# A two-layer hybrid encoder step: another order of projections and heads in the mixer, masks in spare rows, Silu on ScalarE, scaling on GpSimd

## The chip, the cores and the metric

The kernel runs on one core of a Trainium2 chip. The metric is device time in microseconds (us) of one execution. Before the change three runs gave 1753.67 us as median (1753.1 to 1754.33).

## The reference, cut to what matters

320 rows (256 of a prompt, 64 of a running stream) go through two layers. Each layer reads one wide projection of its normalised input and feeds three groups with it:

```
xn = rmsnorm(x, g_mix)
qa, ka, va, ga, ra, bb, cb, hb, qc, kc, vc = split_cols(xn @ w_in)     # 3088 columns
y_a = rmsnorm(gla(qa*48**-.5, ka, va, log_sigmoid(ga@w_g2 + b)/16), g_gla) * silu(ra)
y_b = bb * conv3(cb*hb)
a   = softmax(q1 k1) - lam * softmax(q2 k2)      # q, k: rmsnorm, then rotary; 4 heads x 2 parts
y_c = rmsnorm(a @ vc, g_sub) * (1 - lam_init)    # prompt rows see keys up to their own chunk of 64
x   = x + concat(y_a, y_b, y_c) @ w_out
x   = x + ffn(rmsnorm(x, g_ffn))                 # layer 0: dense SwiGLU; layer 1: top 2 of 8 experts
```

Outputs are the rows, and the keys, values, recurrent states and convolution histories of both streams. All is float32.

## The kernel before, in words

Activations lie transposed: 1024 features in 8 blocks of 128 partitions, 320 tokens in the free dimension (`xR`). Each weight block of 128 columns, a *cut* of 128x1024, is loaded by SyncE into a ring of three slots, split by ScalarE into a rounded high part (`hi`, L757) and by VectorE into the rest (`lo`, L1103). TensorE multiplies three products of high and low parts, 8 blocks by 3 = 24 matmuls of 320 columns (`features`, `three`, L1707 is the matmul helper, L1710 the transpose helper). A cut is made three cuts ahead of its use. A layer has 25 projection cuts and 8 output cuts (`wo_cut`, also 24 matmuls each).

PSUM banks are dealt out as rings whose jobs are listed ahead (`JOBS`): C and T have two banks, S two, O and D one. A job may begin when the job one ring length before it has been emptied. Every engine runs its own list, written out by hand, and all waits are semaphore counts; the order of the lists is the order in `build`.

The mixer of a layer goes, on TensorE: `kc` (3 cuts), `qc` (3), `qa` (2), `ka` (2), `vc` (3), with transposes back to rows (`rows_T`), sums of squares (`square_sums`), the spread of the row norms (`spread_rstd`), the gate logits and the transposes of rotated keys and queries (`heads_T`) between them. Then a loop over 12 heads (3 row tiles by 4 heads) with one projection cut in each round as filling (`FILL`: `va`, `ra`, `bb`, `cb`, `hb`), and rounds that also take a piece of the recurrent group (`inner`, `update`, `recurrent`). A head is `scores` (on TensorE), maximum and its negative (VectorE), two exponentials (ScalarE), the difference of the two softmaxes (VectorE), transpose and product with the values (TensorE). Then the rows of both groups are transposed (`transposed`), gated, split and multiplied with `w_out`.

What the change touches: the mask of the scores was an own matmul of one row, `C("rowsel")` times `C("neg")`, in `scores`. The gate `silu(ra)` was an exponential on ScalarE (`ra_exp`) and add, reciprocal and product on VectorE (`swish`, L1322 to L1324). Rows were scaled by their reciprocal roots on VectorE (`scaled`, L1159); GpSimd only computed the roots (`rsqrt`, L588 and L589) and added the squares of the input (`add_squares`, L595 and L598). `decays` and `decayed` prepare the recurrent group. The gains `g_gla` and `g_sub` were broadcast over partitions with a matmul of one row (`bcast`) and multiplied in row form.

Of the kernel before, what the change touches and what calls it, by code (L numbers as in the profile page):

```python
# [24 lines left out]
P = 128  # L25
# [33 lines left out]
for _name, _w in [("ident", 128), ("tri", 128), ("ones", 128), ("scan", T), ("cc", NT * DK), ("ss", NT * DK),  # L59
                  ("tok", NT), ("iota8", 8), ("slot", MAXB * P), ("attm", H * CH), ("rowsel", P), ("neg", CH)]:  # L60
    CONST[_name] = (_at, _w)
    _at += _w
# [20 lines left out]
for _l in range(DEPTH):  # L83
# [5 lines left out]
    for _n, _c in (("vc", VC), ("va", VA), ("ra", RA)):  # L89
        _unit(("in", _l, _c, 256), [(_n, _l, 0), (_n, _l, 1)])  # L90
        _unit(("in", _l, _c + 256, 128), [(_n, _l, 2)])
    for _n, _c in (("bb", BB), ("cb", CB), ("hb", HB)):
        _unit(("in", _l, _c, 256), [(_n, _l, 0), (_n, _l, 1)])
    for _c in range(2):
        for _j in range(2):
            _unit(("wo", _l, _c, _j), [("wo", _l, _c, 2 * _j), ("wo", _l, _c, 2 * _j + 1)])
# [48 lines left out]
FILL = ["va", "va", "va", "ra", "ra", "ra", "bb", "bb", "cb", "cb", "hb", "hb"]  # L145
JOBS = {r: [] for r in "CTSOD"}
JOBS["T"] += [("par",), ("bcast", 0)]
JOBS["D"] += [("bcast", 1)]
for _k in range(KB):
    JOBS[XT_RING[_k]].append(("xt", _k))  # L150
for _l in range(DEPTH):
    JOBS["C"] += [c[2:] for c in CUTS[KC0[_l]:KC0[_l] + N_IN]]
    JOBS["C"] += [("ya", _l, t) for t in range(NT)] + [("yc", _l, t) for t in range(NT)]
    JOBS["T"] += [("tok", "kc", _l, c) for c in range(3)] + [("tok", "qc", _l, c) for c in range(3)]
    JOBS["T"] += [("pk", _l), ("tok", "vc", _l, 0), ("kt", _l, 0), ("kt", _l, 1), ("kt", _l, 2), ("tok", "vc", _l, 1)]
    JOBS["T"] += [("qt", _l, t) for t in range(NT)] + [("tok", "vc", _l, 2)]
    for _n in range(HEADS + 2):
        if 1 <= _n <= 3:
            JOBS["T"].append(("tok", "va", _l, _n - 1))
        if _n == 2:  # L160
            JOBS["T"] += [("kd", _l, t) for t in range(NT)]
        if _n >= 2:
            JOBS["T"].append(("at", _l, _n - 2))
    JOBS["S"] += [("s", _l, n) for n in range(HEADS)]
    JOBS["O"] += [("oc", _l, t) for t in range(NT)]
    JOBS["D"] += [("ss", 2 * _l), ("R", 2 * _l), ("gl", _l, 0), ("gl", _l, 1), ("att", _l, 0), ("att", _l, 1)]
    JOBS["D"] += [("U", _l, 0), ("U", _l, 1), ("U", _l, 2)] + [("oa", _l, t) for t in range(NT)]
# [59 lines left out]
def build(nc, A, O):  # L227
# [5 lines left out]
    with ExitStack() as ctx:  # L233
# [34 lines left out]
        pcol = sb("pcol", [P, 48])  # L268
        bc = sb("bc", [P, 960])
# [33 lines left out]
        bgla = bc[:, 576:768].rearrange("p (l d) -> p l d", l=DEPTH)  # L303
        bsub = bc[:, 768:960].rearrange("p (l d) -> p l d", l=DEPTH)
# [39 lines left out]
        era = [glaf[:, 3 * T:4 * T], glaf[:, 6 * T:7 * T]]  # L344
        bbs = glaf[:, 4 * T:6 * T].rearrange("p (b n) -> p b n", b=2)
        yv = glaf[:, 6 * T:6 * T + 2 * (T + 2)].rearrange("p (b n) -> p b n", b=2)
        brow, prow = glaf[0:1, 0:960], glaf[0:48, 960:960 + P]
# [5 lines left out]
        atm = mb("atm", [P, 256])  # L353
# [6 lines left out]
        mx = mb("mx", [P, 2, 2])  # L360
        nm = mb("nm", [P, 2, 2])
        sm = mb("sm", [P, 2, 2])
        rc = mb("rc", [P, 2])
        rc2 = mb("rc2", [P, 1])
# [59 lines left out]
        const_in, prow_in, brow_in, x_in, w_small = sem("const_in"), sem("prow_in"), sem("brow_in"), sem("x_in"), sem("w_small")  # L424
# [10 lines left out]
        bcast_ready, tables_ready, lam_exp = sem("bcast_ready"), sem("tables_ready"), sem("lam_exp")  # L435
# [3 lines left out]
        ln_ready, d_ready, exps_ready, gk_ready = sem("ln_ready"), sem("d_ready"), sem("exps_ready"), sem("gk_ready")  # L439
        rope_ready, conv_ready = sem("rope_ready"), sem("conv_ready")  # L440
        era_ready, ya_ready, yc_ready = sem("era_ready"), sem("ya_ready"), sem("yc_ready")
        swish_ready, silu_ready, yhi_ready, ylo_ready = sem("swish_ready"), sem("silu_ready"), sem("yhi_ready"), sem("ylo_ready")
        nm_ready, am_ready = sem("nm_ready"), sem("am_ready")
# [11 lines left out]
        heads_order = [("oc", 0), ("oa", 0), ("oa", 1), ("oc", 1), ("oa", 2), ("oc", 2)]  # L455
# [57 lines left out]
        def _(sp):  # L513
# [15 lines left out]
            sp.wait_ge(const_in, 16)  # L529
            sp.wait_ge(x_in, 32)  # L530
            for l in range(DEPTH):
                sp.dma_start(wga[:, l], A["w_in"][l, :, GA:GA + GR].rearrange("(k p) n -> p k n", p=P)).then_inc(wga_in, 16)
            for n, u in enumerate(UNITS):
                src, (b, w) = source(u)
# [39 lines left out]
        def _(pool):  # L574
# [15 lines left out]

            def add_squares(i, o):
# [43 lines left out]
            pool.wait_ge(bcast_ready, 1)  # L635
            hd = DK // 2
            for l in range(DEPTH):
                for w in range(2):
# [3 lines left out]
                    nc.gpsimd.tensor_tensor(SG[:, l, w, :, hd:DK], ssn[:, :, hd:DK], g[:, 0:hd].unsqueeze(1).to_broadcast([P, NT, hd]), ALU.mult)  # L642
                last = nc.gpsimd.tensor_scalar(bsub[:, l], bsub[:, l], 1.0 - LAM0[l], None, ALU.mult)
# [23 lines left out]
            for l in range(DEPTH):  # L667
# [4 lines left out]
                for what in ("kc", "qc"):  # L672
# [3 lines left out]
                    if what == "kc":  # L676
                        keys_out(l)
                for what, t in heads_order:
                    pool.wait_ge(ss_ready, ss_count(l, what, t))
                    rsqrt(rs_slot(l, what, t), TILES[t][1], DV, 4)  # L680
                    if (what, t) == ("oa", 0):
                        states_out(l)
                    if (what, t) == ("oa", 2):
                        history_out(l)
# [44 lines left out]
        def _(act):  # L729
            step = Steps(act, act_step)  # L730
            hs_n = [0]
            act.dma_start(const[:], A["const"]).then_inc(const_in, 16)
            act.dma_start(xhat[:, 0:2, :], A["x_prompt"][0].rearrange("(t p) d -> p t d", p=P)).then_inc(x_in, 16)
            act.dma_start(xhat[0:DEC, 2, :], A["x_sample"][0]).then_inc(x_in, 16)
            at = 0
            for name in ("g_q", "g_k", "lambda_q1", "lambda_k1", "lambda_q2", "lambda_k2", "g_gla", "g_sub"):
                n = DEPTH * A[name].shape[1]
                act.dma_start(brow[0:1, at:at + n], A[name].rearrange("l d -> (l d)").unsqueeze(0)).then_inc(brow_in, 16)
                at += n

# [33 lines left out]
            nc.scalar.copy(pcol[:], RT.bank(("par",))[:, 0:48]).then_inc(RT.free, 1)  # L774
            act.wait_ge(RT.full, RT.filled(("bcast", 0)))
            nc.scalar.copy(bc[:, 0:480], RT.bank(("bcast", 0))[:, 0:480]).then_inc(RT.free, 1)
            act.wait_ge(RT.free, 2)
# [4 lines left out]
            for o in range(KB):  # L782
                x_square(0, o)

            act.wait_ge(lam_exp, 1)
            nc.scalar.activation(lamt[:], lamt[:], ACT.Exp).then_inc(lam_exp, 1)

            for l in range(DEPTH):
# [32 lines left out]
                def squares_oa(t):  # L821
                    rows = TILES[t][1]
                    act.wait_ge(RD.free, RD.emptied(("oa", l, t)))
                    squares(Ya[0:rows, t], rows)
# [1391 lines left out]
```

## Time and profile before

| quantity | value |
|---|---|
| median of 3 runs | 1753.67 us |
| the profiled execution's own time | 1753.11 us |
| its span, first to last instruction | 1751.2 us |
| TensorE busy, share of the span | 93% |
| VectorE, ScalarE, GpSimd busy | 74%, 56%, 8% |
| mean granted TensorE clock | 0.949 of full |

The span is what the core's instructions cover; the profiled time has 1.9 us around it. Busy TensorE time comes from modelled ends, so what counts is the idle time and the granted clock of each stretch. In the views by stretch the columns are: stretch and its length, then the busy time (and number of instructions) of TensorE, its weight loads, VectorE, ScalarE and GpSimd, then the granted TensorE clock as a share of full speed, the busy share of the DMA engines, and GB/s.

### The profile page before, as it was taken

The page shows a single profiled execution, that of the slowest core. Times are in us where ns is not written, and L with a number is a line of the kernel's source. Part 1 is how long each engine was busy: PE and PEld are TensorE (multiplying, and loading weights), DVE is VectorE, ACT ScalarE, POOL GpSimd, SP SyncE. Part 2 cuts the span into 40 slices and gives each one's busy share as a digit, 9 for nine tenths or more (in the row PEclk, how much of TensorE's full clock was granted, in tenths as well). Part 3 has the DMA queues.
Part 4 walks back from the last instruction along what each step waited for, and adds up shares of the span by engine and source line. Part 5 has one row for each costly group of instructions (what it writes and reads, how often), then busy time and mean ns, then how long its engine had stood idle before and what let it go on. Part 6 is the DMA issues. An engine that isn't in the chain of part 4 may idle for free.

```text
span 1751.2 us, 21767 instructions
## 1 busy us (share of the span) xinstructions
PE 1626.5 (93%) x8526; PEld 1392.5 (80%) x8526; DVE 1291.2 (74%) x1346; ACT 987.4 (56%) x1042; POOL 144.7 (8%) x181
## 2 busy tenths in 40 slices
PE   5979789999987897889999999999999999999994
PEld 3867689999987686768888888888888888888883
DVE  3656756665447376578888888888888888888885
ACT  3443243333334333357777777777777777777772
POOL 5400211000013002100000000000000000000001
PEclk8988889999999797889999999999999999999997
DMA  5322139444433220399999999999999999999993
GB/s 157 105 93 73 52 108 312 145 150 152 156 109 95 84 73 29 128 360 365 359 383 374 358 389 365 365 385 363 373 381 367 370 375 356 389 370 362 386 364 102
DMA packets 230054, 450.13 MB, mean 257 GB/s; under 512 B 10178, under 2 KB 72336, under 8 KB 229952
## 3 DMA queue, kind: packets, MB, share of 16 engines
q1 hardware_dynamic: 214944, 420.64, 67.4%
q10 hardware_dynamic: 10944, 17.13, 2.7%
q0 software_dynamic: 4064, 10.96, 2.0%
q8 instruction: 69, 1.13, 0.3%
q14 instruction: 33, 0.27, 0.0%
HBM read 431.22 MB, written 17.47 MB: 256 GB/s over the span
## 4 chain that ended last, share of the span: by engine, by line
PE 84%; DVE 9%; ACT 3%; issue 1%; DMA 1%; POOL 1%; POOLq 0%; ACTq 0%; SPq 0%; DVEq 0%
PE bank L1707 27%; PE bank L2128 12%; PE bank L2127 12%; PE bank L2132 12%; PE bank L2138 6%; PE bank L2147 6%; PE bank L2141 6%; DVE cut_lo L1103 2%; PE bank L1710 1%; ACT cut_hi L757 1%; PE bank L2156 1%; POOL acc L598 1%; DVE G L1610 0%; DMA xhat<-x_sample 0%; DVE t L1159 0%
## 5 line engine op out<-in xcount | busy, mean ns | idle before, releaser
L1619 DVE TENSOR_TENSOR split_lo<-raw,split_hi 128x2048 fp32r<-128x2048 f32 x336 | 768.2, 2291 | 129.1 <-ACT split_hi L1020 128.2
L1020 ACT CAST split_hi<-raw 128x2048 fp32r<-128x2048 f32 x336 | 640.5, 1910 | 265.7 <-PE bank L2132 167.8
L2127 PE MATMUL bank<-split_hi,xgT_hi 128*128 128x512 f32 x896 | 359.4, 401 | 3.9 <-DVE xgT_lo L1643 3.9
L2128 PE MATMUL bank<-split_hi,xgT_lo 128*128 128x512 f32 x896 | 356.3, 398 | 0.0
L757 ACT CAST cut_hi<-ring 128x1024 fp32r<-128x1024 f32 x124 | 129.1, 1046 | 274.8 <-PE bank L1707 266.1
L1707 PE MATMUL bank<-xT_hi,cut_hi 128*128 128x320 f32 x752 | 250.0, 332 | 0.5 <-DVE xT_lo L1117 0.5
L2132 PE MATMUL bank<-split_lo,xgT_hi 128*128 128x512 f32 x896 | 246.3, 397 | 0.0
L1707 PE MATMUL bank<-xT_hi,cut_lo 128*128 128x320 f32 x752 | 243.1, 323 | 0.0
L1707 PE MATMUL bank<-xT_lo,cut_hi 128*128 128x320 f32 x752 | 242.9, 323 | 0.0
L1103 DVE TENSOR_TENSOR cut_lo<-ring,cut_hi 128x1024 fp32r<-128x1024 f32 x124 | 152.6, 1235 | 115.4 <-ACT cut_hi L757 115.1
L2127 PEld LDWEIGHTS bank<-split_hi,xgT_hi 128*128 128x128 f32 x896 | 169.2, 189 | 43.5 <-DVE xgT_lo L1643 4.3
L2132 PEld LDWEIGHTS bank<-split_lo,xgT_hi 128*128 128x128 f32 x896 | 169.3, 189 | 41.3
L2128 PEld LDWEIGHTS bank<-split_hi,xgT_lo 128*128 128x128 f32 x896 | 169.5, 189 | 39.5
L1707 PEld LDWEIGHTS bank<-xT_hi,cut_hi 128*128 128x128 f32 x752 | 151.3, 201 | 6.0 <-issue 3.0
L1707 PEld LDWEIGHTS bank<-xT_lo,cut_hi 128*128 128x128 f32 x752 | 152.5, 203 | 0.0
L1707 PEld LDWEIGHTS bank<-xT_hi,cut_lo 128*128 128x128 f32 x752 | 152.1, 202 | 0.0
L2138 PE MATMUL bank<-split_hi,hmT_hi 128*128 128x512 f32 x448 | 142.1, 398 | 0.0
L2141 PE MATMUL bank<-split_hi,hmT_lo 128*128 128x512 f32 x448 | 139.1, 391 | 0.0
L2147 PE MATMUL bank<-split_lo,hmT_hi 128*128 128x512 f32 x448 | 121.8, 393 | 0.0
L2141 PEld LDWEIGHTS bank<-split_hi,hmT_lo 128*128 128x128 f32 x448 | 84.1, 188 | 19.8
L2147 PEld LDWEIGHTS bank<-split_lo,hmT_hi 128*128 128x128 f32 x448 | 84.0, 188 | 19.4
L2138 PEld LDWEIGHTS bank<-split_hi,hmT_hi 128*128 128x128 f32 x448 | 82.3, 188 | 16.9
(263 smaller groups left out, 1633.0 us busy)
## 6 DMA issues: line engine op xcount, KB each, us to landing
raw<-moe_w_gate SPq DMA_DIRECT2D x112, 1024.0 KB, 8.2
raw<-moe_w_up SPq DMA_DIRECT2D x112, 1024.0 KB, 7.6
raw<-moe_w_down SPq DMA_DIRECT2D x112, 1024.0 KB, 5.3
ring<-w_in SPq DMA_DIRECT2D x16, 1024.0 KB, 5.3
ring<-ffn_w_gate SPq DMA_DIRECT2D x11, 1024.0 KB, 5.6
ring<-ffn_w_up SPq DMA_DIRECT2D x11, 1024.0 KB, 5.3
ring<-ffn_w_down SPq DMA_DIRECT2D x10, 1024.0 KB, 5.0
ring<-w_out SPq DMA_DIRECT2D x8, 1024.0 KB, 5.0
```

The lines of the kernel that those rows point to most:

```text
L598: nc.gpsimd.tensor_tensor(acc[:], acc[:], sqx[:, o % 2], ALU.add).then_inc(acc_ready, 1)
L757: nc.scalar.copy(split_cut(cut_hi, q), raw_cut(q)).then_inc(cut_hi_ready, 1)
L1020: return nc.scalar.copy(split_hi[:, i % SR, :], raw[:, (i % PR) * PIECE:(i % PR + 1) * PIECE]).then_inc(hi_ready, 1)
L1103: V.tensor_tensor(split_cut(cut_lo, q), raw_cut(q), split_cut(cut_hi, q).bitcast(F32), ALU.subtract).then_inc(cut_lo_ready, 1)
L1619: V.tensor_tensor(split_lo[:, i % SR, :], raw[:, (i % PR) * PIECE:(i % PR + 1) * PIECE], split_hi[:, i % SR, :].bitcast(F32), ALU.subtract ...
L1707: return TE.matmul(out, lhsT, rhs, start=start, stop=stop)
L2127: TE.matmul(o, xgT_hi[:, kk, :], hi[:, c], start=kk == 0, stop=False)
L2128: TE.matmul(o, xgT_lo[:, kk, :], hi[:, c], start=False, stop=False)
L2132: last = TE.matmul(o, xgT_hi[:, kk, :], lo[:, 512 * k:512 * k + 512], start=False, stop=kk == KB - 1)
L2138: TE.matmul(banks[6 + n][:], hmT_hi[:, b, :], hi[:, c], start=b == 0, stop=False)
L2141: TE.matmul(banks[6 + n][:], hmT_lo[:, b, :], hi[:, c], start=False, stop=False)
L2147: last = TE.matmul(banks[6 + n][:], hmT_hi[:, b, :], lo[:, c], start=False, stop=b == FEB - 1)
```

## The change

In the start: the first weight unit is loaded before anything else; only the identity of the constants comes ahead of the input rows, the other constants after them; the two broadcasts and a new transpose of gains (`par2`) move behind the first projection cut; `g_gla` and `g_sub` come as 24 small DMAs on ScalarE's queue and stand as one column per feature (`ycol`). ScalarE squares each input block directly behind its split. In the mixer: `square_sums` and `spread_rstd` move behind a later cut, key and query transposes are interleaved with the cuts of `ka` and `vc`, the third `vc` cut and the transposes of query tiles 1 and 2 go into the loop of heads, the third `ra` cut behind it. Masks are two extra rows of keys and queries (48 to 50). Scaling by reciprocal roots is GpSimd's, in place, and so is the product `qb`; `silu(ra)` is one ScalarE instruction. The maximum comes negated from one reduction, and a head's difference takes one product instead of two. `y_a` is transposed by feature block, gated and split block by block. In layer 0's FFN `square_sums(1)` and `spread_rstd(1)` each move one cut later.

In the loop, `inner` comes in rounds 3 and 4, `update` in 5, 6 and 10, `recurrent` in 7 (tile 2), 8 and 9. Cut to its core (SyncE, GpSimd, ScalarE, then TensorE):

```diff
-FILL = ["va", "va", "va", "ra", "ra", "ra", "bb", "bb", "cb", "cb", "hb", "hb"]
+FILL = [("vc", 2), ("va", 0), ("va", 1), ("va", 2), ("bb", 0), ("bb", 1), ("cb", 0), ("cb", 1), ("hb", 0), ("hb", 1), ("ra", 0), ("ra", 1)]
...
 for n, u in enumerate(UNITS):
+    if n == 1:
+        sp.wait_ge(x_in, 32)
...
+def scaled(slot, rows, groups, a, done):
+    pool.wait_ge(rs_ready, slot + 1)
+    a = a.rearrange("p (g d) -> p g d", g=groups)
+    nc.gpsimd.tensor_tensor(a, a, small_rs[0:rows, slot, 0:groups].unsqueeze(2).to_broadcast([rows, groups, 384 // groups]), ALU.mult).then_inc(done, 1)
...
+for w, name in enumerate(("g_gla", "g_sub")):
+    for k, a, b, d in ((0, 0, 96, 0), (0, 96, 128, 0), (1, 0, 64, 32), (1, 64, 128, 0), (2, 0, 32, 64), (2, 32, 128, 0)):
+        for l in range(DEPTH):
+            r = 6 * w + 3 * l + k
+            act.dma_start(prow2[r:r + 1, a:b], A[name][l:l + 1, d:d + b - a]).then_inc(gains_in, 16)
...
+def swish(b):
+    act.wait_ge(RC.free, RC.emptied(("ra", l, b)))
+    nc.scalar.activation(sraT[:, b], sraT[:, b], ACT.Silu).then_inc(sra_ready, 1)
...
-mm(b[:, c, 0:keys], q, kT[q0:q0 + DK, h, 0:keys], True, False)
-return mm(b[:, c, keys - CH:keys], C("rowsel")[q0:q0 + 1], C("neg")[q0:q0 + 1], False, True)
+return mm(b[:, c, 0:keys], q, kT[ends, h, 0:keys], True, True)
...
 features(RC, ("kc", l, 0), 2 * l)
-square_sums(2 * l)
+if l == 0:
+    pe.wait_ge(gains_in, 16 * 24)
+    tr(RT.begin(pe, ("par2",))[:, 0:12], prow2, 12).then_inc(RT.full, 1)
...
+    for i in range(2):
+        mm(RT.begin(pe, ("bcast", i))[:, 0:288], C("ones", 1), brow[0:1, 288 * i:288 * i + 288], True, True).then_inc(RT.full, 1)
 features(RC, ("kc", l, 1))
 rows_T("kc", 0)
+square_sums(2 * l)
...
+pe.wait_ge(rope_ready, 6 * l + 1)
+heads_T(("kt", l, 0), 0, krope[:, 0])
 features(RC, ("ka", l, 1))
+pe.wait_ge(rope_ready, 6 * l + 2)
+heads_T(("kt", l, 1), 1, krope[:, 1])
 features(RC, ("vc", l, 0))
+pe.wait_ge(rope_ready, 6 * l + 3)
+heads_T(("kt", l, 2), 2, krope[:, 2])
 features(RC, ("vc", l, 1))
 rows_T("vc", 0)
+pe.wait_ge(rope_ready, 6 * l + 4)
+heads_T(("qt", l, 0), 0, qrope[:, 0])
...
+for n in range(HEADS):
+    RS.begin(pe, ("s", l, n))
+    first_half = step.mark(scores(n, 0))
+    if n >= 2:
+        differ_T(n - 2)
+    if n >= 3:
+        attended(n - 3)
+    step.wait(first_half)
+    scores(n, 1).then_inc(RS.full, 1)
+    features(RC, (FILL[n][0], l, FILL[n][1]))
+    if n in (0, 1):
+        rows_T("vc", n + 1)
+        pe.wait_ge(rope_ready, 6 * l + 5 + n)
+        heads_T(("qt", l, n + 1), n + 1, qrope[:, n + 1])
+    if n in (2, 3, 4):
+        rows_T("va", n - 2)
+        pe.wait_ge(gk_ready, 2 * l + 1)
+        decayed_T(n - 2)
...
+ya_T(RS, 0)
+ya_T(RS, 1)
+differ_T(HEADS - 2)
+attended(HEADS - 3)
+features(RC, ("ra", l, 2))
+differ_T(HEADS - 1)
+attended(HEADS - 2)
+ya_T(RT, 2)
+yc_T(0)
+attended(HEADS - 1)
+yc_T(1)
 wo_cut(0, 0)
-wo_cut(0, 1)
-transposed("yc", Yc, yc_ready, 2)
+wo_cut(0, 1, lambda: yc_T(2))                       # between its two halves
...
 features(RC, ("g", 0), 1)
+features(RT, ("u", 0))
 square_sums(1)
-features(RT, ("u", 0))
 features(RC, ("g", 1))
+features(RT, ("u", 1))
 spread_rstd(1)
-features(RT, ("u", 1))
```

## Rows read from the trace of the kernel before

**Rows 1.** The page, busy time, share and instructions of each engine.
```profile
PE 1626.5 (93%) x8526; PEld 1392.5 (80%) x8526; DVE 1291.2 (74%) x1346; ACT 987.4 (56%) x1042; POOL 144.7 (8%) x181
```

**Rows 2.** Busy time by stretch: mixer of layers 0 and 1, then the experts.
```profile
37.00:56.00 19.00, 19.00 (x120) 18.71 (x121) 8.80 (x15) 6.38 (x15) 13.01 (x23) 0.89 0.43 123
56.00:109.25 53.25, 39.50 (x243) 36.22 (x240) 35.52 (x62) 24.85 (x44) 13.95 (x15) 0.87 0.31 83
109.25:144.50 35.25, 31.49 (x180) 27.45 (x179) 13.53 (x30) 10.10 (x30) 0.00 (x0) 0.80 0.30 97
144.50:201.60 57.10, 56.38 (x409) 48.26 (x408) 41.13 (x88) 20.88 (x60) 2.67 (x5) 0.97 0.23 74
201.60:221.30 19.70, 8.89 (x43) 5.67 (x42) 16.91 (x37) 5.56 (x17) 10.36 (x14) 0.59 0.04 9
221.30:238.15 16.85, 16.85 (x101) 16.59 (x102) 7.08 (x10) 4.02 (x7) 1.21 (x2) 0.87 0.22 65
502.90:522.50 19.60, 19.45 (x118) 19.24 (x119) 7.83 (x15) 6.38 (x15) 1.26 (x3) 0.85 0.32 96
522.50:575.90 53.40, 39.93 (x244) 36.87 (x242) 35.52 (x62) 26.02 (x45) 14.82 (x15) 0.88 0.31 83
688.50:705.40 16.90, 16.86 (x100) 16.62 (x101) 7.15 (x10) 4.09 (x7) 1.21 (x2) 0.86 0.01 2
745.00:1751.20 1006.20, 976.02 (x4335) 790.34 (x4334) 857.40 (x539) 716.22 (x535) 29.96 (x22) 0.98 0.98 359
```

**Rows 3.** Timeline of TensorE: start, length, instructions, idle time before and what ended it.
```profile
36.94 1.28 PE L1707 MATMUL bank<-const_sb,acc 128*128 128x1 f32 x6 [7.99 <-POOL acc L598]
92.68 0.52 PE L1710 MATMUL bank<-const_sb,xhat 128*128 128x128 f32 x3 [1.24 <-ACT vc L803]
106.58 1.71 PE L1710 MATMUL bank<-const_sb,xhat 128*128 128x128 f32 x8 [8.39 <-ACT vc L803]
132.87 0.66 PE L1710 MATMUL bank<-const_sb,gla 128*128 128x128 f32 x4 [3.11 <-ACT va L803]
260.72 1.29 PE L1707 MATMUL bank<-const_sb,acc 128*128 128x1 f32 x6 [4.41 <-POOL acc L598]
503.05 1.28 PE L1707 MATMUL bank<-const_sb,acc 128*128 128x1 f32 x6 [4.73 <-POOL acc L598]
```

**Rows 4.** Busy time by stretch behind two of these waits, layer 0.
```profile
93.00:97.00 4.00, 4.00 (x30) 3.76 (x29) 3.90 (x9) 2.16 (x4) 0.00 (x0) 1.00 0.04 4
132.90:137.00 4.10, 3.77 (x14) 2.91 (x15) 0.00 (x0) 1.07 (x4) 0.00 (x0) 0.56 0.61 212
```

**Rows 5.** The chain that ended last, two stretches of projection on TensorE.
```profile
56.24 3.51 PE bank L1707 x24
75.84 7.40 PE bank L1707 x26
```

**Rows 6.** Timeline of TensorE in a head's scores: mask, product, mask.
```profile
117.31 0.43 PE L1707 MATMUL bank<-const_sb 1*128 1x64 f32 x2
117.67 0.49 PE L1707 MATMUL bank<-qkT 48*128 48x128 f32 x2
118.08 0.43 PE L1707 MATMUL bank<-const_sb 1*128 1x64 f32 x2
```

**Rows 7.** Timeline of ScalarE in the start: a DMA issue, table load, first split.
```profile
4.68 0.31 ACTq L738 DMA_DIRECT2D gla<-g_gla  x1
5.32 1.28 ACT L774 ACT_TABLE_LOAD   x1 [5.32 <-issue]
17.28 2.94 ACT L757 CAST cut_hi<-ring 128x1024 fp32r<-128x1024 f32 x3 [3.60 <-DMA ring<-w_in]
```

**Rows 8.** VectorE by line, 0 to 745 us: busy, mean ns | idle before.
```profile
L1323 DVE RECIPROCAL gla<-gla 128x320 f32<-128x320 f32 x6 | 12.9, 2153 | 0.2
```

**Rows 9.** GpSimd by line, 0 to 745 us.
```profile
L598 POOL TENSOR_TENSOR acc<-acc,sqx 128x320 f32<-128x320 f32 x21 | 19.6, 935 | 44.1 <-ACT sqx L771 41.4 <-POOL acc L595 0.2
L589 POOL TENSOR_TENSOR small_rs<-small_ss,half_neg 128x8 f32<-128x8 f32 x8 | 13.2, 1650 | 0.7
L640 POOL TENSOR_TENSOR CG<-const_sb,bc 128x144 f32<-128x144 f32 x4 | 3.0, 744 | 0.0
```

More of the change, by code:

```diff
@@ L929, in _ @@
                     act.wait_ge(RC.full, RC.filled(("yc", l, t)))
-                    nc.scalar.copy(y_hi[:, 5:8, t0:t0 + rows], RC.bank(("yc", l, t)).rearrange("p (k n) -> p k n", k=4)[:, 0:3, 0:rows]).then_inc(yhi_ready, 1)
-                hi(w0 + 3)
+                    for k in range(3):
+                        last = nc.scalar.activation(y_hi[:, 5 + k, t0:t0 + rows], RC.bank(("yc", l, t))[:, 128 * k:128 * k + rows],
+                                                    ACT.Copy, scale=ycol(1, l, k))
@@ L933, in _ @@
+                    last.then_inc(yhi_ready, 1)
+                    if t == 1:
+                        hi(w0 + 3)
                 hi(w0 + 4)
@@ new lines, in _ @@
+                for n in range(HEADS):
+                    job = (FILL[n][0], l, FILL[n][1])
+                    if n in (6, 7):
+                        state(n - 6)
+                    most(n)
+                    if n:
+                        differ(n - 1)
+                    if n == 0:
+                        rope("qc", 2)
+                    if n == 1:
+                        decayed_keys()
+                    if n == 2:
+                        decayed_pairs()
+                    if n in (4, 5):
+                        causal(n - 4)
@@ L1751, in rows_cut @@
                             last = one(i, o, i0 + i == 0)
+                        if i == 0 and between is not None:
+                            between()
                     last.then_inc(cut_used, 1)
@@ L1820, in _ @@
                 rows_T("qc", 0)
+                spread_rstd(2 * l)
                 features(RC, ("qc", l, 2))
@@ new lines, in _, with ya_T @@
+                    if n in (7, 8, 9):
+                        if n == 7:
+                            pe.wait_ge(qb_ready, l + 1)
+                            pe.wait_ge(s0_in, 32 * (l + 1))
+                        recurrent((n - 5) % 3)
+                def ya_T(R, k):
+                    pe.wait_ge(y_normed, 5 * l + 4)
+                    b = R.begin(pe, ("ya", l, k))
+                    for t, (t0, rows) in enumerate(TILES):
+                        last = tr(b[:, t0:t0 + rows], Ya[0:rows, t, P * k:P * k + P], rows)
+                    last.then_inc(R.full, 1)
@@ L2198, in _constants @@
     at("attm")[:] = np.tile((p % CH)[:, None] <= np.arange(CH)[None, :], (1, H))
-    at("rowsel")[:] = p < CH
-    at("neg")[:] = -1e30
+    at("qscale")[:, 0] = np.where(p % HW < DK, SC, 1.0)
+    late = np.arange(P) >= CH
+    for t in range(2):
+        at("kpad")[:, 2 * t + t] = np.where(late, -1e30, 0.0)
+        at("qpad")[:, 2 * t + t] = ~late
     return c
```

637 lines of the change are left out of this document (314 added, 323 removed).

## The prediction, made before the changed kernel ran

> **What bounds the kernel now.** I read the page first, then busy time by stretch, the timeline of TensorE with its waits, and the chain of waits. The page [rows 1] shows TensorE busy for 93% of the span; the reader should not stop there, because a matmul at half clock counts as busy too. The stretches say more [rows 2]. From 745 us to the end the experts run at a granted clock of 0.98 with the DMA engines busy at 0.98: 1006 us that no line of this diff touches. The two mixers are another matter. Layer 0 has a stretch of 53.25 us (from the end of `qc` to the first head) in which TensorE was busy for 39.50 at a clock of 0.87, then 35.25 us (heads 0 to 3) at 0.80, then 57.10 us (heads 4 to 11) at 0.97, then 19.70 us (the two rows' end) with 8.89 busy at 0.59, then 16.85 us (four output cuts) at 0.87. Layer 1 repeats these six stretches within 0.6 us; the first, second and last stand there. The timeline [rows 3] names the waits: 7.99 us for GpSimd's sum of squares in the start, 8.39 before the query transposes, 3.11 among the first heads, 4.41 at the FFN, 4.73 at layer 1.
>
> A wait costs more than its length. Behind the 3.11 us wait the granted clock was 0.56 over the next 4.1 us, behind one of 1.24 us it stayed at 1.00 [rows 3, 4]: these are the 1.2 and the 2.4 GHz level. A projection cut of 24 matmuls takes 3.51 us at the upper level; 26 such instructions behind a wait took 7.40 [rows 5]. So each stretch is bounded by TensorE's order and by what that order waits for, and its work at the upper level is its length times its clock, less its idle time times its clock.
>
> **The change part by part**, against the profiled execution's own 1753.1 us (the median of three runs is 0.6 above it).
>
> *Start, layer 0.* ScalarE issues 23 more DMAs (24 gains and the identity come, two go): 23 x 0.31 = 7.1 us [rows 7]. Its table load thus begins at 12.4 instead of 5.3 and ends at 13.7. The first weight unit is by then loaded, since it no longer stands behind constants and rows; so the first split begins near 14 instead of 17.28: 3 us won. The squares follow each split, so GpSimd's 8 additions of 0.94 [rows 9] run beside the first cut and the 7.99 us wait goes, also because `square_sums` moves one cut back. With it goes the low clock behind it, 19.0 x (1 - 0.89) = 2.1 us [rows 2]. Added are one transpose and two broadcasts, at most half a cut's work: 2 us. Result: 3 + 8 + 2 - 2 = 11 us. What the early unit takes from the input rows' bandwidth is hidden up to ScalarE's 14 us; if that cover went, it is the 3 us. In layer 1 the wait is 4.73 and the clock term 19.6 x 0.15 = 2.9; `square_sums` comes one cut of 3.5 us later, so some 0.6 us of the wait is left: 7 us.
>
> *From `qc` to the first head.* 53.25 x 0.87 = 46.3, less the idle 13.75 x 0.87 = 12.0, is 34.3 us of work at the upper level. The third `vc` cut (3.5) and its and two query tiles' transposes (about 1.5) leave, `spread_rstd` (1) comes: 30.3. Key tiles are transposed as soon as each is rotated; the recurrent group's decays, behind which the queries' copies stood on ScalarE, move behind the first head. What is late next is the copy of query tile 0, which now stands behind a split that waits for the second `vc` cut. Its wait lies between 0 and the 8.39 us of before; by my order of the ScalarE list it is some 2 to 3 us, near the lower end, and I take 2.5: 33 us, 20 won per layer. VectorE was busy for 35.5 us in this stretch; it loses six scalings, the decays, one rotation, one split and one copy to other engines and to the next stretch, about 10 us, so it fits, tightly. GpSimd takes 1.65 us for a tile's roots [rows 9], and its scaling of 384 elements, which no row shows, lies between 0.94 x 384/320 = 1.1 us and three times that, 3.4 (the broadcast product at L640 has a mean of 0.74 for 144 elements). At 1.1 the six tiles take 17 us, at 3.4 they take 31; queries are wanted last near the end of the stretch, so I cost it at nothing and keep up to 3 us for the upper end.
>
> *Heads 0 to 3.* 35.25 x 0.80 = 28.2, less idle 3.76 x 0.80 = 3.0, less eight mask products of 0.36 us (start to start, [rows 6]) = 2.9: 22.3 us. The transposes that come and go are about equal. But the decays (formerly ahead of the heads) and the last rotation now stand on VectorE behind head 0's maximum, and splits on ScalarE behind copies that wait for them. The T ring has two banks, so head 0's transposed difference waits for ScalarE's copy of the third `vc` rows, and head 1's for that of the first `va` rows. That added wait, with its clock, lies between 0 and the 13 us by which the old stretch exceeded its work. I take 9 (two waits of about 3 and one fall of the clock): 31 us, 4 won.
>
> *Heads 4 to 11.* 57.1 x 0.97 less eight more masks (2.9) is 52.5, plus half a microsecond of moved transposes: 53, 4 won. Six reciprocals of 2.15 us [rows 8] leave VectorE, but TensorE hardly waited in this stretch (0.7 us idle), so they are worth nothing here by themselves.
>
> *End of the mixer and four output cuts.* 19.70 x 0.59 + 16.85 x 0.87 = 26.3, less idle 10.81 x 0.59 = 6.4, plus the third `ra` cut 3.5: 23.4 of 36.5. That cut now covers the last heads' differences, and feature blocks 0 and 1 are gated ahead of the rest. Late next is tile 2 of the attention: roots on GpSimd in five steps, product, transposes between the halves of the second output cut. The added wait is between 0 and 13 us; 3 taken: 26.5, 10 won. The Silu table load of 1.28 us [rows 7] is inside these 3. The Trainium skill (ScalarE: Activation LUTs, What ACT_TABLE_LOAD costs) puts a switch of table at 2.66 us, about half of it a drain; the row shows the load alone. By the page the sum would be 2.8 us higher, an estimate, if nothing hid it.
>
> *FFN of layer 0.* The 4.41 us wait and the slow instructions behind it give way to two waits of about 1 us: 3 won.
>
> Sum: layer 0: 11 + 20 + 4 + 4 + 10 = 49; layer 1: 7 + 20 + 4 + 4 + 10 = 45; FFN 3. 1753 - 97 = 1656 for the profiled execution, 1657 as a median.
>
> **The rivals.**
> 1. *VectorE and ScalarE set the pace of the shortened stretches.* VectorE's 35.5 us against 53.25 speaks for it, and the scaling that returns to its list through a GpSimd at its upper price; its 13.5 busy of 35.25 us among the first heads speaks against. Then the second stretch gives 15 instead of 20, heads 0 to 3 nothing, the end 3: 33 + 29 + 3 = 65 us, 1688. Each new wait would drag the clock down again. The Trainium skill (TensorE: Matmul & The Clock Gate, HAM oscillation) tells of kernels that fall back to the low rate at every wait for data; the 3.11 us row agrees, the 1.24 us row shows a wait that did not do it.
> 2. *The new order leaves no wait.* Every stretch falls to its work: 11 + 23 + 13 + 4 + 13 = 64, layer 1 60, FFN 4: 1625. For it: the cuts are all split three ahead. Against: the bank rings named above.
> 3. *Slower: the clock stays at the lower level through the mixers.* The place is the loop of heads with its many short waits. At the lower level a cut costs up to 0.8 of itself more (about 6.4 for 3.51, [rows 5]). The two mixers hold 2 x (30 + 22 + 53 + 23) = 256 us of work; if all waits went (128 won) but more than 128/0.8 = 160 of the 256 us ran at the lower level, the kernel would be slower; at 200 us it takes 1785. Against: 57 us with short waits ran at 0.97 [rows 2].
>
> **How the numbers follow.** Forecast 1657 (its own range 1640 to 1680): 0.55. Rival 1 (1680 to 1715): 0.25. Rival 2 (1615 to 1640): 0.13. A gain smaller than rival 1's: 0.03. Rival 3: 0.04. The range 1630 to 1708 leaves out half of rival 2, the upper end of rival 1 and the last two. A measurement tells 0.2% (3.5 us) from no change; below that lie all but 0.05: faster 0.95, same 0.01, slower 0.04.
>
> **What would show it.** Right: no wait of TensorE above 1 us between the first cut and the sum of squares; the stretch from the end of `qc` to the first score near 33 us; heads 0 to 3 near 31 with waits for ScalarE's copies; no mask products; `y_a` done before the last heads; the experts' 1006 us unchanged. Wrong: waits of TensorE on rotations (rival 1, with GpSimd's scaling above 3 us), heads 0 to 3 below 25 us (rival 2), or a granted clock below 0.7 in heads 4 to 11 (rival 3).

## The result, and where the time went

The changed kernel takes 1647.39 us (median of 4 runs, 1644.33 to 1651.6), the kernel before 1753.76 on the same chip (4 runs, 1753.1 to 1754.33): ratio 0.9396, 95% interval 0.9385 to 0.9407. 1657 was forecast, 1630 to 1708 as range. By medians 106.4 us are gone, where 97 were forecast. The execution profiled is the slowest of the four: it took 1651.6 us with a span of 1649.8, and 101.4 us of span are gone.

The page, busy time, share and instructions of each engine, answers to [rows 1]:

```profile
PE 1582.9 (96%) x8463; PEld 1358.9 (82%) x8463; DVE 1247.7 (76%) x1262; ACT 994.8 (60%) x1068; POOL 177.1 (11%) x224
```

VectorE's busy time fell by 43.5 us, GpSimd's rose by 32.4; TensorE's fell by 43.6, though it executes nearly the same work (63 instructions fewer, 32 of them masks): much of it had run at the lower clock, as the clock column of [rows 2] shows. The stretches of the changed kernel, in the order of [rows 2] and with the same columns (stretch, busy time of TensorE, its weight loads, VectorE, ScalarE, GpSimd, then the granted clock, the DMA share and GB/s):

```profile
29.50:50.36 20.86, 20.86 (x118) 19.74 (x119) 8.72 (x18) 8.48 (x20) 9.38 (x18) 1.00 0.52 149
50.36:82.99 32.63, 30.93 (x211) 29.01 (x209) 27.08 (x54) 18.30 (x34) 25.54 (x28) 1.00 0.40 113
82.99:107.42 24.43, 22.97 (x173) 20.63 (x173) 17.03 (x34) 15.03 (x43) 2.23 (x1) 1.00 0.46 144
107.42:164.19 56.77, 56.28 (x407) 48.99 (x407) 34.08 (x72) 22.79 (x64) 10.77 (x17) 0.94 0.21 68
164.19:172.38 8.19, 8.19 (x55) 6.32 (x54) 6.57 (x12) 5.93 (x12) 2.64 (x5) 1.00 0.36 130
172.38:188.10 15.72, 14.72 (x102) 14.42 (x101) 8.93 (x19) 7.21 (x16) 7.27 (x13) 1.00 0.25 20
464.53:497.15 32.62, 30.92 (x210) 29.01 (x209) 26.04 (x50) 19.57 (x35) 21.63 (x21) 1.00 0.40 112
588.05:603.80 15.75, 14.74 (x103) 14.44 (x102) 8.92 (x19) 7.21 (x16) 7.26 (x13) 1.00 0.05 11
644.00:1649.80 1005.80, 974.97 (x4331) 789.71 (x4329) 856.93 (x539) 716.21 (x535) 29.86 (x22) 0.98 0.98 359
```

The second row is the stretch that took 53.25 us at a clock of 0.87; it now takes 32.63 with 1.70 us idle at 1.00. The experts' row is unchanged. Set against the steps of the prediction, all from this trace and the one of before (the stretches of layer 1 are cut at the same instructions; heads 0 to 3 end with the last product of `inner(0)`, which in layer 0 of the kernel before is at 144.17 us, 0.33 ahead of the row in [rows 2]):

| step, us won | forecast | layer 0 | layer 1 |
|---|---|---|---|
| start, to the end of the second `qc` cut | 11 / 7 | 56.0 to 50.36: 5.6 | 24.3 to 17.2: 7.2 |
| from there to the first score | 20 | 53.25 to 32.63: 20.6 | 53.4 to 32.6: 20.8 |
| heads 0 to 3, to the end of `inner(0)` | 4 | 34.9 to 24.4: 10.5 | 35.5 to 26.0: 9.5 |
| heads 4 to 11 | 4 | 57.43 to 56.77: 0.7 | 57.44 to 56.71: 0.7 |
| end and four output cuts | 10 | 36.55 to 23.9: 12.6 | 36.5 to 23.95: 12.6 |
| FFN, to the end of layer 1's first cut | 3 | 0.9 | |

TensorE's waits above 0.35 us from 36 to 230 us (timeline: start, length, instructions, idle time before and what ended it), against [rows 3]:

```profile
82.99 1.00 PE L1769 MATMUL bank<-qkT 50*128 50x128 f32 x4 [1.70 <-ACT qkT L861]
94.48 0.30 PE L1772 MATMUL bank<-const_sb,am 128*128 128x128 f32 x1 [0.38 <-ACT vc L850]
100.75 0.30 PE L1772 MATMUL bank<-const_sb,am 128*128 128x128 f32 x1 [0.90 <-ACT va L850]
178.91 0.37 PE L1772 MATMUL bank<-const_sb,xhat 64*128 64x64 f32 x3 [1.00 <-DVE y_lo L1519]
199.21 0.41 PE L1769 MATMUL bank<-y_hi,cut_hi 128*128 128x320 f32 x1 [0.37 <-DVE cut_lo L1177]
205.06 0.38 PE L1769 MATMUL bank<-xT_hi,cut_hi 128*128 128x320 f32 x1 [2.06 <-DVE cut_lo L1177]
214.11 0.78 PE L1769 MATMUL bank<-const_sb,acc 128*128 128x1 f32 x6 [1.29 <-POOL acc L622]
225.63 0.39 PE L1769 MATMUL bank<-xT_hi,cut_hi 128*128 128x320 f32 x1 [1.20 <-DVE gR L1565]
```

The waits of 7.99, 8.39, 3.11 and 4.41 us are gone, and none here is as long as 2.1 us. The wait at 205.06 is new and was in no step of mine: it is for a weight cut, whose load came late (e9).

### The profile page after: what moved, and what is told of

The parts are those of the page before. It is cut to its first block, busy times and chain, and to the rows that moved or that the text cites. A ratio compares the mean times of both kernels' runs of the same rounds, so it can differ in the third digit from the quotient of the medians.

```text
span 1649.8 us, 21672 instructions
## 1 busy us (share of the span) xinstructions
PE 1582.9 (96%) x8463; PEld 1358.9 (82%) x8463; DVE 1247.7 (76%) x1262; ACT 994.8 (60%) x1068; POOL 177.1 (11%) x224
## 4 chain that ended last, share of the span: by engine, by line
PE 90%; DVE 3%; DMA 3%; ACT 2%; POOL 1%; issue 1%; ACTq 0%; POOLq 0%; DVEq 0%
PE bank L1769 30%; PE bank L2215 13%; PE bank L2216 13%; PE bank L2220 13%; PE bank L2226 6%; PE bank L2235 6%; PE bank L2229 6%; PE bank L1772 2%; PE bank L2244 1%; DMA ring<-ffn_w_up 1%; ACT cut_hi L800 1%; DVE cut_lo L1177 1%; DMA xhat<-x_sample 1%; POOL acc L622 1%; DMA raw<-expert_rows,pos 1%
## 5 line engine op out<-in xcount | busy, mean ns | idle before, releaser
L1769 PE MATMUL bank<-xT_hi,cut_hi 128*128 128x320 f32 x752 | 245.0, 326 | 5.5 <-DVE xT_lo L1191 2.2
L1769 PE MATMUL bank<-xT_hi,cut_lo 128*128 128x320 f32 x752 | 236.9, 315 | 0.0
L1769 PE MATMUL bank<-xT_lo,cut_hi 128*128 128x320 f32 x752 | 236.7, 315 | 0.0
L1769 PEld LDWEIGHTS bank<-xT_hi,cut_hi 128*128 128x128 f32 x752 | 146.3, 195 | 14.0 <-issue 7.0
L1769 PEld LDWEIGHTS bank<-xT_lo,cut_hi 128*128 128x128 f32 x752 | 146.8, 195 | 0.0
L1769 PEld LDWEIGHTS bank<-xT_hi,cut_lo 128*128 128x128 f32 x752 | 146.6, 195 | 0.0
```

The lines of the kernel that those rows point to most:

```text
L1769: return TE.matmul(out, lhsT, rhs, start=start, stop=stop)
```

## The experiments

Each is an edit of the changed kernel and is compared with it through the ratio to the kernel before. Two such ratios can be told apart from about 0.2% (3.5 us) on.

### The masks put back (e1)

```diff
+mm(b[:, c, 0:keys], q, kT[ends, h, 0:keys], True, False)
+return mm(b[:, c, keys - CH:keys], C("rowsel")[q0:q0 + 1], C("neg")[q0:q0 + 1], False, True)
-return mm(b[:, c, 0:keys], q, kT[ends, h, 0:keys], True, True)
```

> The changed kernel with sixteen mask products per layer put back beside the spare rows (the mask is then added twice, which changes no output). Theory (TensorE's order sets the time in the heads): each costs its start-to-start time, 0.36 us in the kernel before, so 2 x 16 x 0.36 = 11.5 us more than the changed kernel's 1647.4, about 1659, of which half falls into heads 0 to 3 and half into heads 4 to 7. Rival (the chain score, maximum, exponential, difference sets the pace and TensorE has slack there): under 3 us more.

1661.38 us, ratio 0.9475 (0.9459 to 0.949): 14 us more, with 11.5 inside the uncertainty of about 3. Rival out: TensorE has hardly any slack in the heads. Half and half was wrong. From the start of one cut to that of the next, two masks of 0.36 us cost 0.71 to 0.73 us in heads 1 and 4 to 7, but 0.37 in head 2 and 0.01 in head 3. There the changed kernel waits 0.38 and 0.90 us for ScalarE's copies (94.48 and 100.75 in the timeline above); in e1 the first wait is gone and the second 0.19 us. So a removed instruction counts with its start-to-start time where TensorE would not have waited anyway: with 0.72 for head 0, 1.8 us in heads 0 to 3 and 2.9 in heads 4 to 7, 9.4 in two layers. A slow cut at head 7 in both layers of this trace (5.31 instead of 3.76 us) adds 3.1.

### Scaling back on VectorE (e2), reciprocals back on VectorE (e3)

```diff
-scaled(rs_slot(l, what, t), rows, 8, (krow if what == "kc" else qrow)[0:rows, t], qk_normed)      # GpSimd
+step(V.tensor_tensor(v, v, small_rs[...].to_broadcast([rows, 8, DK]), ALU.mult))                  # VectorE, in rope
```

> The changed kernel with the scaling of keys and queries by their roots back on VectorE (six products of some 0.55 us per layer; GpSimd keeps the roots). Theory (TensorE's order sets the time, VectorE was busy for 27.1 of the 32.6 us between the end of the second qc cut and the first score and has room for 3.3 more): within 3 us of 1647.4. Rival 1 of the prediction (VectorE sets the pace of this stretch): 2 x 6 x 0.55 = 6.6 us more or above, and a wait of TensorE for a rotation appears.

1649.33 us, 0.9408 (0.9393 to 0.9424): no difference. The stretch before the first head is 32.46 us in both layers, as in the changed kernel (32.47 and 32.46, from the spread of the roots to the first score). Rival 1 is out for this stretch, and the move of these six products to GpSimd was worth nothing by itself. The scaling of the outputs' rows was not put back.

```diff
+if 4 <= n < 10:
+    V.reciprocal(t1[:, 0:T], Rb[:])
```

> The changed kernel with six reciprocals of 128x320 per layer added on VectorE, one behind the difference of each of the heads 3 to 8, to a scratch tile that nobody reads: the load that the Silu on ScalarE took from VectorE. Theory (TensorE hardly waits there; VectorE busy for 34 of 56.75 us, with them 47): under 3 us more than 1647.4, so that this part of the change was worth nothing by itself. Rival 1 (VectorE in its order sets the pace): up to 2 x 6 x 2.15 = 26 us more.

1651.4 us, 0.9423 (0.9407 to 0.9439): 4 to 5 us more, a little over my bound, of the 25.8 us that VectorE now spends on them (VectorE by line, with busy time and mean ns):

```profile
L1473 DVE RECIPROCAL t<-Rb 128x320 f32<-128x320 f32 x12 | 25.8, 2153 | 0.4
```

One wait of TensorE appears that the changed kernel has not (TensorE's timeline):

```profile
117.58 1.15 PE L1771 MATMUL bank<-va,kdn 64*64 64x96 f32 x16 [0.75 <-DVE att L1409]
```

So VectorE's load there is hidden but for a fifth of it at most: the masking of the inner scores (L1409) comes late behind the added work. The addition and the product that the Silu also replaced were not put back.

### The start (e4)

```diff
-for q in range(CR): hi(q)                 # ScalarE
+for q in range(CR - 1): hi(q)             # hi(CR - 1) behind the eight input blocks
...
-for q in range(2): lo(q)                  # VectorE
+lo(0)                                     # lo(1), lo(2) behind the eight input blocks
```

> The changed kernel with ScalarE's third split moved behind the eight input blocks, and VectorE's low half of the second cut too. Theory (the start lost its gain because ScalarE, in order, stood 2.59 us for the second weight unit ahead of the first input block, and VectorE did a low half that is wanted only by the second cut): the first matmul of the first cut starts near 18.1 instead of 21.0 us, and the kernel takes 2 to 3 us less, about 1645. Rival (the start is bound further on, by the arrival of constants and gains behind the first cut or by GpSimd's sum of squares): the first cut starts earlier, a wait of as much appears behind it, and the time stays at 1647.4.

1645.76 us, 0.9383 (0.9367 to 0.9398): by the time not told apart from 0.9396, so what follows is read from the traces. ScalarE in the start, first in the changed kernel, then with the edit:

```profile
12.68 1.28 ACT L817 ACT_TABLE_LOAD   x1 [12.68 <-issue]
...
14.20 1.99 ACT L800 CAST cut_hi<-ring 128x1024 fp32r<-128x1024 f32 x2
18.78 1.04 ACT L800 CAST cut_hi<-ring 128x1024 fp32r<-128x1024 f32 x1 [2.59 <-DMA ring<-w_in]
19.73 0.56 ACT L806 ACTIVATE xT_hi<-xR,pcol 128x320 fp32r<-128x320 f32 x1
```

```profile
14.23 2.00 ACT L800 CAST cut_hi<-ring 128x1024 fp32r<-128x1024 f32 x2
17.05 0.56 ACT L806 ACTIVATE xT_hi<-xR,pcol 128x320 fp32r<-128x320 f32 x1 [0.82 <-DVE xR L1185]
```

The first split came at 14.20, as forecast, but the first input block stood behind the third split, and that behind a DMA. With the edit the first cut starts at 18.8 instead of 21.0 us. In this trace about 1.5 of the 2.2 us were given back: the second cut ran partly at the lower rate (5.3 us for 24 matmuls instead of 3.76). The rate is also what makes the profiled start of the changed kernel a long one. Matmuls of the second cut in the changed kernel, then in e2, whose start is the same code:

```profile
32.63 0.47 PE L1769 MATMUL bank<-xT_hi,cut_hi 128*128 128x320 f32 x1
32.90 0.47 PE L1769 MATMUL bank<-xT_hi,cut_lo 128*128 128x320 f32 x1
33.16 0.47 PE L1769 MATMUL bank<-xT_lo,cut_hi 128*128 128x320 f32 x1
```

```profile
32.61 0.31 PE L1769 MATMUL bank<-xT_hi,cut_lo 128*128 128x320 f32 x1
32.76 0.31 PE L1769 MATMUL bank<-xT_lo,cut_hi 128*128 128x320 f32 x1
32.91 0.31 PE L1769 MATMUL bank<-xT_hi,cut_hi 128*128 128x320 f32 x1
```

0.27 against 0.15 us from start to start. The spread of the roots starts at 50.5 us in the changed kernel's profile and between 45.9 and 47.9 in nine other profiles with the same start (e1 to e3, e5 to e10). With the edit it comes at 45.2 here and at 43.5 and 43.6 in e11 and e12, whose second cut ran at the upper rate: in the traces the theory holds, at 2.3 us or a little more, where the clock does not take it back.

### The order ahead of the first head (e5, e6)

```diff
 rows_copy("vc", 0, vc)                       # ScalarE
+act.wait_ge(d_ready, 2 * l + 2)
+decay_exp(ed, ed, 1/16); decay_exp(eq, d1, 1/16); decay_exp(ek, d1, -1/16); decay_exp(eb, cum, 1/16)
 heads_copy("qt", 0, qT)
```

> The changed kernel with the four exponentials of the recurrent group's decays put back in front of the copy of query tile 0 on ScalarE (as in the kernel before, where the queries' copies stood behind them). Theory (the 8.39 us wait before the first head came from this order: VectorE ends the decays' differences at 87, then four exponentials of 0.73): the wait of 1.70 us before the first score becomes some 7 to 9 us per layer, with a fall of the clock behind it, 14 to 20 us more in all, 1662 to 1668. Rival (the queries' copies are late anyway, for the rotations or the second vc cut): under 4 us more.

1666.58 us, 0.9509 (0.9492 to 0.9527): 19 us more. ScalarE waits for VectorE's decays and then does the four exponentials; TensorE waits for the copy that follows. The timeline of ScalarE, then of TensorE:

```profile
83.05 2.61 ACT L914 ACTIVATE gla<-gla 128x640 f32<-128x640 f32 x4 [3.37 <-DVE gla L1314]
85.57 0.56 ACT L861 COPY qkT<-bank 128x512 f32<-128x512 f32 x1
```

```profile
86.27 1.61 PE L1766 MATMUL bank<-qkT 50*128 50x128 f32 x4 [8.99 <-ACT qkT L861]
```

The wait is 8.99 us, close to the 8.39 of [rows 3]: this one order on ScalarE was that wait. Layer 1 has 10.27 us where the kernel before has 7.03, so the 19 us are a little more than the old order cost.

```diff
 heads_T(("qt", l, 0), 0, qrope[:, 0])        # TensorE; ScalarE and VectorE likewise
+features(RC, ("vc", l, 2))
+for t in (1, 2):
+    rows_T("vc", t); heads_T(("qt", l, t), t, qrope[:, t])
```

> The changed kernel with the third vc cut, the rotation of query tile 2 and the transposes of query tiles 1 and 2 back in front of the first head; head 0 has no cut. Work is moved, none added. Theory (the gain before the first head came from taking waits out, and a cut beside each head hides the chain of score, maximum, exponential and difference): 2 to 4 us per layer more, since heads 0 and 1 stand without a cut between them and the first score waits for query tile 2's copy; 4 to 8 us in all, 1651 to 1655. Rival (only the decays' place mattered, not the queries'): within 2 us of 1647.4.

1645.48 us, 0.9392 (0.9374 to 0.9409): no difference, theory out. The stretch before the first score grows from 32.46 to 37.07 us, and the one from there to `inner(0)` falls from 22.9 and 24.5 to 19.5 and 18.2. What is moved is paid where it stands; head 0 does without a cut beside it. So 4.6 of the 20 us per layer won before the first head are this work, which is paid again among the heads.

### Groups inside the cuts (e7, e10)

```diff
-features(RC, job); inner / update / recurrent of this round
+features(RC, job, between=...)               # the group between blocks 3 and 4 of the cut
```

> The changed kernel with the recurrent group's products of each head (inner, update, recurrent) moved from behind the head's cut into its middle. No work is added. Theory (the clock falls behind 4 to 5 us of small products in a row without a wait, at 108, 153 and 566 us, each about 2.4 us long; shorter rows of small products keep it up): the three slow cuts go, 5 to 7 us less, about 1641. Rival A (the falls lie where they lie by chance, and move): as many slow cuts, within 2 us of 1647.4. Rival B (half a cut earlier the products wait for their inputs): new waits of TensorE, slower than 1649.

1665.61 us, 0.9503 (0.9488 to 0.9519): 18 us more, rival B. Half a cut earlier the groups wait for VectorE's masking of the inner scores, and slow cuts follow (TensorE's timeline):

```profile
110.05 0.91 PE L1769 MATMUL bank<-gla 48*64 48x64 f32 x8 [1.56 <-DVE att L1409]
...
118.72 1.15 PE L1769 MATMUL bank<-va,kdn 64*64 64x96 f32 x16 [1.36 <-DVE att L1409]
```

The recurrent products of heads 7 to 9 waited for nothing, so they were tried alone (the same edit for `n in (7, 8, 9)`):

> The changed kernel with the recurrent products of heads 7 to 9 alone moved into the middle of those heads' cuts; inner and update products stay behind theirs (moved too, they waited 1.56 and 1.36 us for the copy of the inner scores). Theory (the fall of the clock at 153 and 566 us comes behind 5 us of small products in a row; half cuts between them keep it up): the slow cut of head 10 goes in both layers, 2 x 1.5 to 2.4 us, about 1643 to 1644.5. Rival (the falls move): within 1 us of 1647.4.

1647.98 us, 0.9412 (0.9393 to 0.9432): no difference, though the mechanism is there. Around head 10's cut, first the changed kernel, then e10:

```profile
148.00:160.00 12.00, 11.88 (x96) 10.53 (x95) 6.59 (x15) 5.04 (x14) 4.31 (x5) 0.86 0.28 96
```

```profile
145.00:157.00 12.00, 11.88 (x101) 10.34 (x99) 7.97 (x18) 5.24 (x16) 4.29 (x6) 1.00 0.45 161
```

Head 10's cut took 4.9 to 6.2 us in both layers of the changed kernel, e9 and e12, and 3.76 in both layers of e10 and e11. With e1 to e6 and e8, which have the same products ahead of that cut, it was slow in 18 of 20 places and took 3.76 us in two (layer 0 of e2, layer 1 of e8): behind such a run of small products the clock mostly fell, not always. But a group inside a cut no longer runs beside the next head's score: heads 7 and 8 take 0.6 us more each (e11 against e9: 7.35 and 8.29 us from one cut to the next, against 6.76 and 7.63), head 9 0.3. What the clock gives back (1.2 us at head 10) that takes.

### The last `ra` cut one place earlier (e8)

```diff
+features(RC, ("ra", l, 2))
 ya_T(RS, 0); ya_T(RS, 1); differ_T(HEADS - 2); attended(HEADS - 3)
-features(RC, ("ra", l, 2))
```

> The changed kernel with the third ra cut moved ahead of the transposes of y_a and of the difference of head 10, so that it no longer stands between the last two differences. Work is moved, none added. Theory (this cut is the cover for the last head's difference; the kernel before stood 13 us there): a wait of 2 to 4 us before the difference of head 11 and a clock fall behind it, 5 to 10 us more in two layers, 1652 to 1657. Rival (the end gained only because the stretch has other transposes and the gating is ahead): within 2 us of 1647.4.

1649.87 us, 0.9418 (0.9399 to 0.9437): 2 to 4 us more, at the edge of what can be told apart and below the theory's 5 to 10, which is out. In layer 0 one wait of 0.53 us appears and one of 1.00 becomes 1.41; there is none of 2 to 4 us. The last differences are ready nearly early enough without that cover. Which of the other edits at the end (transposes by feature block, blocks 0 and 1 gated ahead) took away the old 10.8 us of idle time was not taken apart.

### The small outputs earlier (e9)

```diff
+if (what, t) == ("oc", 2):                    # GpSimd, ahead of the last attention tile's roots
+    history_out(l); states_out(l)
...
-states_out(l); history_out(l)                 # behind all roots
```

> The changed kernel with the eight small outputs of a layer (four of the states, four of the convolution's history, strided by columns) issued by GpSimd ahead of the last attention tile's roots, some 10 us earlier, as it idles there for 7.8 us, and not behind them. Theory (in the changed kernel these outputs run beside the load of the first FFN weight unit: issued at 181.9 us it is split at 199.9 only, 18 us later, where its issue took 5.3 us to landing before; so the FFN starts behind a wait of 2.06 us, and the FFN's 3 us were not won): the unit lands sooner, the wait of TensorE near 205 us goes, and the kernel takes 2 to 3 us less, about 1645. Rival (the unit is late because its slot is freed late, or because the ring's other loads share the queues): the wait stays, within 1 us of 1647.4.

1644.87 us, 0.9383 (0.9369 to 0.9397): the interval overlaps the changed kernel's, but the trace shows the step itself. DMA issues of 178 to 202 us, KB each and median us to landing; the changed kernel, then e9:

```profile
ring<-ffn_w_gate SPq DMA_DIRECT2D x2, 1024.0 KB, 12.6
ring<-ffn_w_up SPq DMA_DIRECT2D x1, 1024.0 KB, 15.1
...
out<-up POOLq DMA_DIRECT2D x4, 1.0 KB, 8.4
```

```profile
ring<-ffn_w_up SPq DMA_DIRECT2D x2, 1024.0 KB, 5.4
ring<-ffn_w_gate SPq DMA_DIRECT2D x1, 1024.0 KB, 5.3
```

The wait at 205 us is gone, and from the first output cut to layer 1's spread the trace has 287.7 us instead of 292.3. In ten profiles without this edit (the changed kernel, e1 to e8 and e10) the stretch takes 291.6 to 294.2, in three with it (e9, e11, e12) 287.7 each time. The theory holds, at 4.6 us of the stretch; the median shows 2.5. Whether the states or the history hold up the loads was not taken apart.

### Versions that put edits together (e11, e12)

e11 has the edits of e4, e6, e9 and e10 at once, e12 those of e4 and e9:

```diff
+e4: hi(CR - 1), lo(1), lo(2) behind the input blocks    # e11, e12
+e9: history_out(l); states_out(l) ahead of ("oc", 2)    # e11, e12
+e6: vc 2, query tiles 1 and 2 ahead of head 0           # e11
+e10: recurrent(...) between blocks 3 and 4, n in (7, 8, 9)   # e11
```

> The changed kernel with four edits at once: third split and second low half behind the input blocks; queries 1 and 2 and the third vc cut ahead of the first head; recurrent products of heads 7 to 9 inside the cuts; the small outputs ahead of the last attention tile's roots. Theory (each takes its own piece and what the first three win in layer 0 is no longer given back at the FFN's first weight unit): 1.6 + 2 + 3 + 2.5 = about 9 us less than 1647.4, 1638 to 1641. Rival (layer 0's gains are given back at the FFN, whose weights come when they come): half of it, 1643 to 1645.

1639.14 us, 0.935 (0.9331 to 0.9368): faster than the changed kernel by 0.46%, intervals apart; 1638 to 1641 was expected.

> The changed kernel with two edits alone: third split and second low half behind the input blocks, and the small outputs ahead of the last attention tile's roots. Theory (in the traces of the kernel with four edits the stretches from the spread of the roots to the output projection are as long as without its two reorderings, 112.9 and 113.5 us, so its gain is 4.6 us at the FFN and about 2 at the start): the same time as with four edits, 1639 to 1642. Rival (the reorderings before and among the heads bring part of it): 1643 or more.

1642.18 us, 0.9366 (0.9353 to 0.9379): faster than the changed kernel too, at the border between theory and rival and not told apart from e11. What the two reorderings bring beside the other two edits stays open; between them lie 3 us. The best version measured is e11.

## Why the prediction was right

**The frame held.** Each stretch fell to nearly its work at the upper level, and the end moved by the sum of the stretches; the experts took 997.5 us from their first matmul to the end in both traces. Put back one at a time, the masks (14 us), the decays' order (19) and the reciprocals (4 to 5) make up some 38 of the 106 us. The rest, above all the starts, the wait for the gate logits (below) and the end, is read from waits that are gone in the trace; no run put it back.

**That the sum came so near is in part luck.** In the profiled execution heads 0 to 3 and the end won 17 us more than forecast, and the start of layer 0, heads 4 to 11 and the FFN 14 us less. By medians the gain is 10 us above the forecast; some 4 of these are the start, which this execution had slower than the others.

**Before the first head**, 20 forecast and 20.6 and 20.8 found. Layer 0's 13.75 us of idle time became 1.70. Of it 8.39 is the decays' place on ScalarE (e5), 1.24 the wait for a copy in [rows 3], and 3.97 a wait that [rows 3] does not list, before the second gate logits (TensorE's timeline in the kernel before):

```profile
75.84 1.40 PE L1707 MATMUL bank<-gla,wg 64*128 64x320 f32 x2 [3.97 <-DVE gla L1223]
```

There VectorE emptied the bank of the first logits (L1223) behind the scaling and rotation of a key tile, a copy and a low half, from 71.3 to 75.2 us. In the changed kernel the scaling is GpSimd's and the others come behind L1223's successor (L1297) in VectorE's list, and the wait is gone in both layers; no run put this order back. The wait that I put in the place of the old one (2.5 us for the copy of query tile 0) was there with 1.70. GpSimd's scaling of 384 elements took 1.50 us for query tiles, near the lower end of my bounds, and 0.93 for key tiles, below them (by line and shape, busy time and mean ns, 0 to 745 us); e2 shows that it costs nothing on either engine:

```profile
L612 POOL TENSOR_TENSOR va<-va,small_rs 128x384 f32<-128x384 f32 x4 | 6.0, 1502 | 0.3
...
L612 POOL TENSOR_TENSOR qkT<-qkT,small_rs 128x384 f32<-128x384 f32 x4 | 3.7, 934 | 0.3
```

**Heads 0 to 3** were the mis-sized term: "two waits of about 3 and one fall of the clock", 9 us. The waits for the copies of the third `vc` rows and the first `va` rows are there, but take 0.38 and 0.90 us, and the cuts behind them took 3.6 us, so the clock stayed up. The one fall came in layer 1, behind the 1.70 us before the first score, and cost 1.6. So 10.5 and 9.5 us were won, not 4. I had taken the value in the upper part of its bounds; rival 2, for which these waits are nothing, was nearer in this stretch. Layer 0's 24.4 us is even below the 25 that the prediction names as the sign of rival 2, layer 1's 26.0 is above.

**Heads 4 to 11** gave 0.7 in each layer instead of 4. The masks are worth their 2.9 (e1), but the sum left the clock at its old 0.97 or better. It is at 0.94, with two slow cuts in layer 0 (5.3 us each) and one of 6.2 in layer 1, none of them behind a wait; the kernel before has one of 5.25 in each layer. e10 and e11 show that the one at head 10 goes when the small products ahead of it are split up.

**The start of layer 0** gave 5.6 in the profiled execution. The wait of 7.99 us went. Of the step "the first split begins near 14 instead of 17.28: 3 us won" the split's time was right, its being the last thing to wait for was wrong: the third split and its DMA came next (e4). The 2.1 us for the low clock were not won in this execution, but in others of the same code, where the spread comes 2.6 to 4.6 us sooner; there the step is worth 8 to 10 (these executions are e1 to e3 and e5 to e10).

**The end** gave 12.6 instead of 10: the wait for attention tile 2 was 1.00 and not 3 us. TensorE was busy through the whole stretch of the Silu's table load (1.28 us at 165.29, the first activation at 166.59), so the load cost nothing. The Trainium skill (ScalarE: Activation LUTs, What ACT_TABLE_LOAD costs) has 2.66 us for a switch, about half of it a drain. Here the load begins 0.01 us behind the split ahead of it and ends 0.02 us before the activation, so this trace shows no drain on either side of it.

**The FFN** gave 0.9 instead of 3. The old wait went, but transfers collided: GpSimd now issues the states from 177.4 and the history from 179.7 us, and SyncE the first FFN unit at 181.9 (e9). I had followed POOL's queue for the roots only, not for the outputs that stand behind them.

Of the rivals, 1 (VectorE and ScalarE set the pace) falls with e2 and is a few us with e3; 3 did not come, as the mixers ran at 0.93 to 1.00. The row of 26 instructions behind a wait in [rows 5], on which rival 3 draws, was read too simply: two of them are the gate logits above, and the cut behind them took 5.89 us, part of it at the upper level. A whole cut at the lower level, 24 matmuls 0.27 us apart as in the second cut here, is the 6.4 us that was used.

## What to carry to other kernels

Where one engine is busy for 93%, cut its time into stretches, take idle time out of each, and weigh the rest by the clock: that sum was right within 5 us of 101 in the profiled execution and within 10 of 106 by medians, while most of its single terms were off by 2 to 6 us in both directions. Of what a change moves, follow the small DMAs as well as the work: eight small outputs, moved behind other work, cost as much as the wait that was removed. Moving work off VectorE was worth nothing (six scalings per layer, e2) or 4 to 5 us (six reciprocals per layer, e3); one group of exponentials moved behind a copy was worth 19.

## What the runs showed that was not expected

- **Rows of the clock in the first 37 us.** The granted clock reads 1.00 for the whole start, in the stretch 29.50:50.36 too, while matmuls there are 0.27 us apart, as at the lower level; other executions of the same code have 0.15. In the start only the spacing tells the rate.
- **The same wait, two outcomes.** Behind 1.70 us before the first score the next cut took 3.76 us in layer 0 and 5.32 in layer 1 (the stretches behind it, layer 0 first):

```profile
84.00:89.00 5.00, 4.94 (x34) 4.57 (x34) 4.93 (x10) 1.76 (x8) 0.00 (x0) 1.00 0.68 210
498.00:504.00 6.00, 6.00 (x33) 5.83 (x31) 5.90 (x12) 1.48 (x6) 0.00 (x0) 0.72 0.57 175
```

- **VectorE and GpSimd side by side.** The low part of an input block takes 0.54 us on VectorE in the kernel before, 0.75 beside GpSimd's additions of squares; GpSimd's scaling takes 0.83 us at 55 and 59 us and up to 1.84 at 74, beside VectorE's rotations.
- **Small outputs** (four of 36 KB, and four of 1 KB strided by columns that take 8.4 us to landing) beside loads of 1 MB: the loads take 12.6 and 15.1 us instead of 5.3.
